# A hybrid attention layer: x transposed by the host, 512-wide chunks, and heads projected in pairs

## What is computed

```python
h = einsum('bnd,de->bne', x, w_in)            # 1024 -> 3328
qa, ka, va, ga, qb, kb, vb, gb = split(h)     # widths 512 x4, 512, 128, 128, 512
# A: 8 heads, rotary q and k, windows (128,1), (512,4), (2048,16) mixed by their denominators
out_a = dilated_attention(rope(qa), rope(ka), va) * silu(ga)
# B: 8 q heads, 2 kv heads, RMS-normalised q and k, 2-D axial rotary, dense attention
out_b = gqa_attention(axial_rope(rms(qb)), axial_rope(rms(kb)), vb) * silu(gb)
f = einsum('bne,ed->bnd', concat(out_a, out_b), w_out)
y = layer_norm(2 ** 0.25 * x + f, ln_g, ln_b)
```

## Time and profile before

| | |
|---|---|
| time, three runs | 473.42, 475.0, 477.52 us; median 475.0 |
| span of the profiled execution | 474.6 us |
| busy | TensorE 438.0 us (92%), its weight loads 413.2 (87%), VectorE 301.4 (64%), GpSimd 248.1 (52%), ScalarE 230.7 (49%) |
| mean granted clock of TensorE | 0.983 of full speed |
| moved by DMA | 30.00 MB |

### The profile page before, as it was taken

How to read it: one execution, slowest core, us unless ns; L and a number is a source line. 1 busy time by engine, 2 the same in 40 slices (tenths; PEclk the granted TensorE clock), 3 DMA queues, 4 the chain that set the end, 5 groups by cost and what they waited for, 6 DMA issues and landing times.

```text
span 474.6 us, 8965 instructions
## 1 busy us (share of the span) xinstructions
PE 438.0 (92%) x3292; PEld 413.2 (87%) x3292; DVE 301.4 (64%) x826; ACT 230.7 (49%) x519; POOL 248.1 (52%) x340
## 2 busy tenths in 40 slices
PE   1999979998899999999999999999999789999990
PEld 1999969987799999998899999999888678999990
DVE  1543675339987788664577877855586777433664
ACT  3332113335456565666565565655675876121222
POOL 1126953795554746334346565653543773454664
PEclk9999989999899999999999999999999989999997
DMA  6611212110200101102010010110200136231222
GB/s 237 255 45 52 71 35 74 39 46 23 68 23 23 46 23 36 56 24 66 14 54 23 24 46 24 40 51 23 68 1 23 44 111 245 88 95 42 78 100 89
DMA packets 23291, 30.00 MB, mean 63 GB/s; under 512 B 1872, under 2 KB 19408, under 8 KB 23248
## 3 DMA queue, kind: packets, MB, share of 16 engines
q1 hardware_dynamic: 22816, 29.30, 19.0%
q10 hardware_dynamic: 432, 0.13, 0.1%
HBM read 26.28 MB, written 3.15 MB: 62 GB/s over the span
## 4 chain that ended last, share of the span: by engine, by line
PE 66%; POOL 10%; DVE 10%; issue 7%; ACT 3%; DMA 2%; SPq 1%; ACTq 0%; DVEq 0%; POOLq 0%
PE bank L504 15%; PE bank L505 15%; PE bank L506 15%; PE bank L465 9%; PE bank L593 6%; POOL scr L1062 3%; DVE prob L870 2%; PE bank L551 2%; PE bank L552 2%; DMA h<-x_prompt 2%; DVE tmp_s L796 1%; POOL tanh L1048 1%; ACT prob L707 1%; DVE p_lo L878 1%; POOL w_lo L1032 1%
## 5 line engine op out<-in xcount | busy, mean ns | idle before, releaser
L504 PE MATMUL bank<-w_hi,t_lo 128*128 128x256 f32 x576 | 168.2, 292 | 1.9 <-DVE nmax L870 0.8
L506 PE MATMUL bank<-w_hi,t_hi 128*128 128x256 f32 x576 | 164.0, 285 | 0.0
L505 PE MATMUL bank<-w_lo,t_hi 128*128 128x256 f32 x576 | 163.9, 285 | 0.0
L504 PEld LDWEIGHTS bank<-w_hi,t_lo 128*128 128x128 f32 x576 | 111.5, 194 | 3.1 <-DVE nmax L870 1.0
L505 PEld LDWEIGHTS bank<-w_lo,t_hi 128*128 128x128 f32 x576 | 111.6, 194 | 0.1
L506 PEld LDWEIGHTS bank<-w_hi,t_hi 128*128 128x128 f32 x576 | 111.3, 193 | 0.0
L1032 POOL TENSOR_TENSOR w_lo<-raw,w_hi 128x512 fp32r<-128x512 f32 x52 | 67.2, 1302 | 59.2 <-ACT w_hi L659 59.1
L1113 POOL TENSOR_SCALAR prob<-prob,den 128x512 f32<-128x512 f32 (+1 forms) x96 | 60.5, 635 | 68.6 <-DVE den L899 68.5
L707 ACT ACTIVATE prob<-prob,nmax 128x512 f32<-128x512 f32 (+1 forms) x96 | 62.3, 649 | 54.1 <-DVE nmax L870 53.6
L878 DVE TENSOR_TENSOR p_lo<-bank,p_hi 128x512 fp32r<-128x512 f32 x80 | 54.8, 685 | 3.0 <-ACT p_hi L716 2.2
L659 ACT ACTIVATE w_hi<-raw 128x512 fp32r<-128x512 f32 x62 | 37.6, 622 | 34.6 <-DMA raw<-w_in 17.4
(11 more groups left out here) (97 smaller groups left out, 784.3 us busy)
## 6 DMA issues: line engine op xcount, KB each, us to landing
raw<-w_in SPq DMA_DIRECT2D x50, 256.0 KB, 2.8
raw<-w_out SPq DMA_DIRECT2D x16, 256.0 KB, 2.9
h<-x_prompt SPq DMA_DIRECT2D x7, 512.0 KB, 6.8
h<-x_sample SPq DMA_DIRECT2D x4, 512.0 KB, 9.6
y_prompt<-h SPq DMA_DIRECT2D x8, 256.0 KB, 2.1
y_sample<-h SPq DMA_DIRECT2D x4, 256.0 KB, 2.1
cst<-consts SPq DMA_DIRECT2D x1, 960.0 KB, 9.5
h<-x_prompt SPq DMA_DIRECT2D x2, 256.0 KB, 3.8
```

The lines of the kernel that those rows point to most:

```text
L504: nc.tensor.matmul(out, a_lo, b_hi, start=(m == 0), stop=False)
L505: nc.tensor.matmul(out, a_hi, b_lo, start=False, stop=False)
L506: ins = nc.tensor.matmul(out, a_hi, b_hi, start=False, stop=(m == KT - 1))
```

## The change

The kernel is written anew around the same arithmetic.

- The host hands over x transposed (`xt`), weights cut into units of 512 KB in the order of use (`weight_units`), and tables for both rotations. TensorE transposes no x; `x_high` and `x_low` split 768 columns of a contraction slice at a time.
- B's q (chunk 0, 512 wide), kv (chunk 1, 256 wide) and A's values (chunk 2, 512 wide) run ahead of the loop with the contraction outermost: for each slice k all six tiles, in six of the eight banks (`natural`).
- The other columns come in 16 blocks of 128 (`BLOCKS`: a pair of A's q or k heads, or a pair's gates), projected with columns on partitions, 512 and then 256 tokens wide (`fill`), spread over steps 0 to 75 by `FILL_AT`: a fifth of a block a step, from step 40 on 0.229.
- A's q/k need no transposes: `rotate` shuffles partitions out of the bank and multiplies, GpSimd adds (`add_turned`). B is transposed in pairs of heads (five pairs, 30 transposes, the first four batches ahead of the loop). Heads are split from SBUF (`stage_high`, `stage_low`); VectorE doubles the keys.
- The gate is kept apart and multiplied in by pair (`apply_gate`, GpSimd; the last on VectorE); `mix` becomes one operation.
- Reciprocal roots: a root on ScalarE, then VectorE.
- The output is 512 wide in 12 items over 8 banks; the first three start in steps 77 to 83.

```diff
-CW = 256
...
+CW = 512
...
+BLOCKS = ("q0", "k0", "q1", "k1", "g4", "g5", "g6", "g7", "q2", "k2", "q3", "k3", "g0", "g1", "g2", "g3")
...
+FILL_AT = ((0, 0.0), (40, 8.0), (75, 16.0))
...
+OUT_AT = {77: (0,), 78: (1,), 79: (2,), 80: (3,), 81: (4,), 82: (5,), 83: (6,)}
...
+            def natural(chunk, k):
...
+                if chunk == 0:
+                    pe.wait_ge(xt_lo, k + 1)
...
+                for t in range(TILES):
+                    i = TILES * chunk + t
+                    if k == 0 and i >= 8:
+                        pe.wait_ge(act_evacuated, i - 8 + 1)
+                    ins = three(bank[i % 8][:, 0:width], x_cols(k, slice(t * P, (t + 1) * P)), w, k == 0, k == KT - 1)
...
+            def fill(b, part, k):
...
+                cols = slice(0, SEQ) if part == 0 else slice(SEQ, TOK)
+                ins = three(acc[part][:, 0:cols.stop - cols.start], weight(g, k, P), x_cols(k, cols),
+                            k == 0, k == KT - 1)
...
-            def x_transposes(t):
...
+            def output(n, m):
+                c, t = out_items[n]
...
+                e = SPLIT_ORDER[m]
+                ins = three(out_bank(n)[:], x_cols(e, slice(t * P, (t + 1) * P)), weight(g, m % 2, CW),
+                            m == 0, m == KT - 1)
...
+            for k in range(KT):
+                natural(2, k)
+                if k == 5:
+                    pe.wait_ge(ident_loaded, 16)
+                    t_batch(0)
+                if k == 6:
+                    t_batch(1)
+            t_batch(2)
+            t_batch(3)
...
+            weights_high(6)
+            for t in range(TILES):
+                evacuate(0, t)
+            weights_high(7)
+            square_root(0)
+            weights_high(8)
+            for t in range(TILES):
+                evacuate(1, t)
+            weights_high(9)
+            square_root(1)
+            weights_high(10)
...
+            t_copy(0)
...
+            for t in range(TILES):
+                evacuate(2, t)
+            t_copy(2)
+            t_copy(3)
+            stage_high(("q", 0))
...
+            def norm_and_rotate(chunk, t):
...
+                    dve.wait_ge(rstd_ready, chunk + 1)
...
+                if n >= 2:
+                    dve.wait_ge(b_rope, n - 1)
+                p_c, p_s = (heads_of(products[:, a, n % 2, 0:m * HEAD_DIM]) for a in range(2))
+                nc.vector.tensor_tensor(p_c, heads_of(src), cos[:, k, None, :].to_broadcast([P, m, HEAD_DIM]), ALU.mult)
+                for a, z in ((0, HALF), (HALF, 0)):
+                    ins = nc.vector.tensor_tensor(p_s[:, :, a:a + HALF], heads_of(src)[:, :, z:z + HALF],
+                                                  sin[:, k, None, a:a + HALF].to_broadcast([P, m, HALF]), ALU.mult)
...
+            def stage_low(e):
...
+                nc.vector.tensor_tensor(by_tile(lo), src, by_tile(hi.bitcast(F32)), ALU.subtract).then_inc(staged_lo, 1)
+
+            def double_keys(j):
...
+                nc.vector.tensor_copy(k_st[complement(rows), kv % 2], k_st[rows, kv % 2].bitcast(F32)) \
+                    .then_inc(keys_doubled, 1)
...
             def mix(g):
...
                 dve.wait_ge(low_copied, g + 1)
-                o = o_lo[rows, :]
-                after(nc.vector.tensor_tensor(o, o_ps[0:HEAD_DIM, 0:2 * P], o, ALU.add))
-                gate = mix_t[rows, head_columns(j)[3], 2 * P * k:2 * P * (k + 1)]
-                nc.vector.tensor_tensor(gate, o, gate, ALU.mult).then_inc(mixed, 1)
...
+                nc.vector.tensor_tensor(mix_t[rows, mix_row(j), 2 * P * k:2 * P * (k + 1)], o_ps[0:HEAD_DIM, 0:2 * P],
+                                        o_lo[rows, :], ALU.add).then_inc(mixed, 1)
...
+            def rotate(b, part):
...
+                nc.vector.stream_shuffle(turn[:, 1, cols], src, SWAP)
+                nc.vector.tensor_tensor(turn[:, 0, cols], src, cos_a[:, 0:w], ALU.mult).then_inc(acc_freed, 1)
+                dve.wait_ge(acc_freed, 2 * b + part + 1)
+                nc.vector.tensor_tensor(turn[:, 1, cols], turn[:, 1, cols], sin_a[:, 0:w], ALU.mult) \
+                    .then_inc(a_products, 1)
...
+            weights_low(7)
+            for t in range(TILES):
+                norm_and_rotate(0, t)
+                sums(1, t)
+                if t == 2:
+                    weights_low(8)
+            mean_square(1)
+            head_rstd(1)
+            weights_low(9)
+            for t in range(TILES):
+                norm_and_rotate(1, t)
...
+            def residual(n):
...
                                                      op0=ALU.mult, op1=ALU.add))
-                nc.vector.bn_stats(stats[:, t, c, :], r).then_inc(dve_evacuated, 1)
-                if c == OUT_CHUNKS - 1:
-                    dve.wait_ge(*evac[i])
-                    nc.vector.bn_aggr(mv[:, t, :], stats[:, t, :, :]).then_inc(stats_ready, 1)
+                ins = nc.vector.bn_stats(stats[:, t, c, :], r)
+                if c == 0:
+                    ins.then_inc(out_freed, 1)
+                else:
+                    after(ins)
+                    v, y, z, tmp = (lnr[:, t, a:a + 1] for a in (0, 1, 2, 3))
+                    rs, shift = (lnr[:, t, a:a + 1] for a in (4, 5))
+                    after(nc.vector.bn_aggr(mv[:, t, :], stats[:, t, :, :]))
+                    nc.vector.tensor_scalar(v, mv[:, t, 1:2], 1.0, LN_EPS, ALU.mult, ALU.add).then_inc(var_ready, 1)
+                    dve.wait_ge(ln_rooted, t + 1)
+                    after(nc.vector.reciprocal(z, y))
+                    after(newton(rs, tmp, v, z))
+                    nc.vector.tensor_scalar(shift, mv[:, t, 0:1], rs, -1.0, ALU.mult, ALU.mult).then_inc(ln_rstd, 1)
...
+            def add_rotation(chunk, t):
...
+                pool.wait_ge(b_products, n + 1)
+                nc.gpsimd.tensor_tensor(dst, products[:, 0, n % 2, 0:w], products[:, 1, n % 2, 0:w], ALU.add) \
+                    .then_inc(b_rope, 1)
...
+            def add_turned(b, part):
...
+                if i == 0:
+                    pool.wait_ge(t_written, len(batches))
+                pair = int(BLOCKS[b][1])
+                if pair >= 2 and part == 0:
+                    pool.wait_ge(staged_lo, staged(N_HEADS_B + 2 * (pair - 2) + 1))
...
+            def apply_gate(m):
...
+                pool.wait_ge(acc_freed, 2 * b + 2)
+                pool.wait_ge(mixed, mixed_through(last_head(e)))
+                nc.gpsimd.tensor_tensor(mix_t[:, e, :], mix_t[:, e, :], gate[:, m % 2, :], ALU.mult).then_inc(gated, 1)
...
+            for t in range(TILES):
+                add_rotation(0, t)
+                square(1, t)
+            for t in range(TILES):
+                add_rotation(1, t)
...
+    xt = np.concatenate([x_prompt, x_sample]).T.reshape(KT, P, TOK).transpose(1, 0, 2)
```

More of the change, by code:

```diff
@@ new lines, in weight, with hi_count, on_dve, lo_taken @@
+        def weight(g, row, width, col=0, cols=None):
+            at = row * width + col
+            n = cols or width
+            hi, lo = unit_places(g)
+            return tuple(a[at // 512][:, at % 512:at % 512 + n] for a in (hi, lo))
+        def hi_count(g, half=1):
+            return half + 1 if g == 0 else g + 2
+        def on_dve(g, half=0):
+            return (g == 0 and half == 0) or NAT_UNITS > g >= 5 or (g >= FIRST_OUT + 3 and g % 2 == 0)
+        def lo_taken(g, half=1):
+            order = [(0, 0), (0, 1)] + [(n, 1) for n in range(1, UNITS_W)]
+            upto = order[:order.index((g, half)) + 1]
+            mine = on_dve(g, half)
+            return (w_lo_dve if mine else w_lo_pool), sum(1 for n, s in upto if on_dve(n, s) == mine)
@@ new lines, in build, with quanta_at, done_at @@
+        ends, total = [], 0.0
+        for b, part, k in quanta:
+            total += SHARE[part] / (KT * sum(SHARE))
+            ends.append(total)
+        def quanta_at(u):
+            lo, hi = blocks_before(u) + 1e-6, blocks_before(u + 1) + 1e-6
+            return [q for q, end in zip(quanta, ends) if lo < end <= hi]
+        def done_at(u):
+            return [(b, part) for b, part, k in quanta_at(u) if k == KT - 1]
+        own_kv = [j == 0 or head_kv(j) != head_kv(j - 1) for j in range(HEADS)]
@@ L400, in group_of, with by_tile, complement, batch_bank @@
+        def by_tile(flat):
+            return flat.rearrange("p (t c) -> p t c", c=P)
+        def complement(rows):
+            return slice(HEAD_DIM - rows.start, P - rows.start)
+        batches = [(n, part) for n in range(1 + N_HEADS_B // 2) for part in range(2)]
+        SPREAD = 4
+        def batch_bank(n):
+            return s_ps[n % 2] if n < SPREAD else t_ps
+        def batches_at(u):
+            return [n for n in range(SPREAD, len(batches)) if n - SPREAD == u]
         def group_of(u):
@@ new lines, in gate_step, with gate_on_dve, rows_of @@
+        def gate_step(m):
+            b = gates[m]
+            ready = next(u for u in range(STEPS) if (b, 1) in done_at(u))
```

(21 more changed lines are left out.)

1308 lines of the change are left out of this document (636 added, 672 removed).

## The result

The changed kernel takes **470.07 us** (median; 469.46 to 470.68), the kernel before beside it 476.17: ratio 0.987, 95% interval 0.983 to 0.991. So it is faster, by 6 us and not by the 29 that I forecast, and outside the range 431 to 461. The profiled execution has a span of 468.0 us.

The account below looks back on a forecast made before the run. TensorE was taken as the bound, until VectorE or a chain of waits is late. Start, chunks, waits, 310.7 us of loop and output work, 13 allowance and 10.4 end summed to 445.9, forecast 446 us; range 431 to 461.

Parts of the forecast that it names:

- TensorE's work: Whole kernel: products and transposes fall from 423.5 to 394.6 us, 28.9 us less, called the surest term.
- The start: Ahead of the first product: it comes at 7.5 us instead of 13.5, bounds 6 and 10.
- the change of chunks: Between chunks 0 and 1: TensorE waits 1.9 us for ScalarE's rounding and evacuations, bounds 0.5 and 3.
- B's chain: Before B's first transposes: VectorE and GpSimd alternate, 4.3 us a tile; TensorE waits 10.3 us, plus 1.6 for the clock.
- The idle time ahead of the first score: Entry into the loop: 3.3 us idle for query head 0's evacuation, copies, rounding and remainder, plus 1.5 for the clock.
- The shuffle: In VectorE's rotation of q and k blocks: taken as 0.685 us for 512 columns, lower bound 0.42.
- that rival: Output tiles: roots and normalization exchange tables, a load for each, giving 455 us; chance 0.07.
- loop allowance 13 us (bounds 5 and 26): Loop and output: time over 310.7 us of work; 5 for steps 40 to 57, 2 first twenty, 5 last ten, 1 clock.
- End 10.4: Behind the last product: 10.4 us instead of 10.9, with VectorE's output tile barely keeping up with TensorE.
- VectorE paces all rotating steps: Rival for the loop's rotating steps: VectorE paces them at 83%, 13 us more, 459 us; chance 0.15.
- The mark: Sign to look for in the loop: VectorE over 90% busy in steps 40 to 57.
- the start of the output: End of the loop: 5 us for the ten last steps; last gate, rounding and remainder (4.1) hidden under 4.8 of output products.

Follow-up runs that it names:

- the kernel with the tail changed: The changed kernel with the bias add over the second half of a row's 1024 columns made by GpSimd instead of VectorE, for all row tiles but the last: 466.12 us.

## Why the prediction failed, step by step

**Right.** TensorE's work (28.9 us less) and its prices. The start: 7.5 forecast, 8.1 measured. The wait at the change of chunks: 1.9 forecast, 1.1. B's chain: its place, its releaser and its cause; the wait is 7.7 us long where I had 10.3, with B's first transposes at 95.1 (95.9 forecast). A tile of it took 4.05 us against my 4.3. The idle time ahead of the first score: 3.3 forecast, 2.7. The shuffle, which no row of before showed: 745 ns for 512 columns and 449 for 256, where I took 685 and had 420 as the lower bound; the rate of the Trainium skill (VectorE: DVE Perf Modes, The perf-mode tier table) had given an estimate of 0.7, and this trace agrees. No table load within the output's tiles: a root takes 0.20 us there and only one load, at 415.24, stands ahead of the first, so that rival falls, and the rule of the Trainium skill (ScalarE: Activation LUTs, Table sets: the hidden batching unit) that the cheap functions are in every set holds in this trace.

**Wrong: the term "loop allowance 13 us (bounds 5 and 26)".** It came out at 34. I worked it out from VectorE's load per step, as if the order of a step were what it had been. The change also moves the transposes of the probabilities behind the projections; I had not laid the two loops' calls side by side, and no sentence of the prediction prices that move. With it put back the same stretch, from 108.8 to 434.7, has 15 us over the work, so the allowance of 13 was about right for the loop that I thought I was pricing, and the kernel took 450.6, inside the range. By the prediction's prices (an estimate) 6.5 of the 15 lie in steps 0 to 74, where I allowed 7, and 9 behind them, where I allowed 6: the second part came out too small. The sum could have held it. The prediction's own step has 1.67 to 1.90 us of block in 3.05 to 3.28. By the late order the copies get one step less its values, 0.48: 2.6 to 2.8 us. They need four transposes (0.44), a rounding of 0.6 (0.38 for 256 columns, more for 512) and a remainder of 0.685: 1.7 with nothing in front of them, and a maximum, a mix or a rotation of 0.4 to 2.5 us in front of the remainder makes them late. With the transposes first, another step's 1.7 to 1.9 us of block lie in between, and cover it.

**Wrong: the term "End 10.4".** It was 14.0. "VectorE's tile there is some 5.4 us of work to TensorE's 5.45, so it barely keeps up" counted VectorE's passes, but not that its last add can end only behind GpSimd's multiply; the tile took 6.23. With that add away the stretch is 10.2.

**Wrong as a mechanism, near as a number: the rival "VectorE paces all rotating steps", 459.** The mark did come: in steps 40 to 57, from 241.22 to 304.75 us, VectorE is busy for 57.94 of 63.53 us, 91%. But there TensorE is busy too, for 61.05; the round window that covers most of these steps:

```profile
240.00:300.00 60.00, 58.26 (x371) 51.22 (x370) 53.42 (x126) 40.18 (x85) 41.31 (x43) 1.00 0.11 36
```

Steps 40 to 57 took 63.5 us and with early transposes 61.4: 2 of the 17 us. The first twenty, where I allowed 2 us, and the last 17, of gates alone, took 67.5 and 62.0 and lost 5 and 6 of them (62.5 and 56.2 with early transposes). So the busiest steps of VectorE lost the least. The steps of gates alone took 3.65 us each (3.31 with early transposes): one of the prediction's signs of being wrong, steps longer than 3.6 us where no block rotates, did come.

**Priced too low: the start of the output**, where I allowed 5 us for the ten last steps and took the last gate, rounding and remainder as hidden: 7.5 us of idling from 367 to 384, 5.7 of them for GpSimd's low part, and low clock beside it (0.80).

**Small: span for time.** I set the two equal. The profiled execution took 469.93 us with a span of 468.0, so 1.9 of the 24 us missing are no part of the kernel's stages.

What stays open: of the 5.5 us of busy time in the loop about 2 are clock by the estimate above, and the rest is unexplained. That the place of the transposes starts all of it is shown by the one edit that takes it away. That it acts through the time left to the two copies is shown for TensorE's wait of 9.5 us; for the other waits that go with it, it is only likely.

## What to carry to other kernels

Where a loop is software-pipelined by hand, list its calls in order for both kernels before pricing any of them, and for each value that goes through two other engines write down the time that the order leaves it and the time that it takes: a margin under 1 us on the mean, with other work in those queues, held 18 of 48 groups here, and the order that gave 2.3 us took 19 us less. VectorE's busy time told nothing of this: it was 302 us with the loss and 299 without. In a tail, count for each pass what it waits for, not only the passes.

## What the hardware showed that was not expected

VectorE's passes with both operands in SBUF, the working memory, mostly get longer when they start while GpSimd works, and those with an operand in PSUM, the memory of TensorE's banks, do not. In the kernel with the tail changed, timelines of both engines:

```profile
457.77 1.52 POOL L1271 TENSOR_TENSOR h<-h,q_b 128x512 f32<-128x512 f32 x1 [2.55 <-ACT h L890]
```

```profile
456.76 0.68 DVE L1129 TENSOR_TENSOR h<-h,q_b 128x512 f32<-128x512 f32 x1
...
458.44 1.41 DVE L1129 TENSOR_TENSOR h<-h,q_b 128x512 f32<-128x512 f32 x1 [0.27 <-ACT h L890]
```

The same multiply took 0.68 us and, started 0.67 us into GpSimd's, 1.41; it depends on nothing that GpSimd makes. In the changed kernel 22 of the remainders `p_lo`, with one operand in PSUM, start inside a two-input pass of GpSimd and take 0.69 us on average, as all 80 do; the one of 161.35 shown above started 0.13 us into a pass of 1.27. The Trainium skill says so (SBUF — State Buffer, Who interferes with whom): a VectorE instruction with two SBUF inputs contends with a GpSimd instruction that reads SBUF, since its second input comes through the read interface that the two share, and the shared pair is an exclusive lock. These traces agree: the multiply of 458.44 ends 0.56 us behind GpSimd's, most of a pass of its own. The sines' product shows it most: cut to 8 columns it still takes 0.44 us on average, and 1.06 beside a remainder of GpSimd:

```profile
157.30 2.55 POOL L1158 TENSOR_TENSOR w_lo<-raw,w_hi 128x512 fp32r<-128x512 f32 x2 [2.80 <-ACT w_hi L717]
```

```profile
157.56 1.06 DVE L1029 TENSOR_TENSOR turn<-turn,cst 128x8 f32<-128x8 f32 x1
```

At 512 columns it took 1.07 on average where I priced 0.685. The prediction allowed for such holding up only in a bound of B's chain, and priced the rotations in the loop as if VectorE were alone.
